# A hybrid decoder layer on one core: the mixers' steps between the projections' half chunks put in another order

## The reference, cut to what matters

```python
h = rmsnorm(x, g_mix_pre)
proj = jnp.einsum('bld,de->ble', h, w_in)                 # 2048 -> 7184 columns
# group B: causal width-4 convolution and SiLU on q, k, v; l2norm of q, k; then, in chunks
A  = jnp.where(strict, bi * jnp.einsum('bhtd,bhsd->bhts', ki, ki) * gam, 0.0)
sol = lax.linalg.triangular_solve(eye + A, rhs, left_side=True, lower=True, unit_diagonal=True)
u  = sol[..., :DV] - jnp.einsum('bhtd,bhde->bhte', sol[..., DV:], S)
S_new = exp(b_last) * S + einsum('bhsd,bhse->bhde', ki * exp(b_last - b), u)
# for the 8 decode tokens the chunk has length 1 and S is one of 8 x 8 stored 128 x 128 states
# group A: gated linear recurrence with a decay per key channel, 8 x 4 stored decode states
x = x + rmsnorm(einsum(concat([oa, ob, oc]), w_out), g_mix_post)
x = x + rmsnorm((silu(h2 @ w_gate) * (h2 @ w_up)) @ w_down, g_ffn_post)
```

## Time and profile before

| | us |
|---|---|
| Median of three runs | 1503.8 |
| The profiled execution: its own time / its span | 1502.13 / 1500.6 |
| PE busy, matmuls (share of the span) | 1423.8 (95%) |
| VectorE busy | 854.1 (57%) |
| ScalarE busy | 661.3 (44%) |
| GpSimd busy | 166.8 (11%) |
| Mean granted TensorE clock | 0.973 of full speed |

### The profile page before, as it was taken

One profiled execution on the slowest core, in us unless ns is written; L12 is line 12 of the kernel. 1 busy time (PEld: TensorE's weight loads), 2 busy tenths in 40 slices (PEclk: granted clock), 3 DMA queues, 4 the chain that ended last, 5 costly groups with the idle time before them and its releaser, 6 DMA issues.

```text
span 1500.6 us, 28229 instructions
## 1 busy us (share of the span) xinstructions
PE 1423.8 (95%) x11389; PEld 1402.2 (93%) x11389; DVE 854.1 (57%) x1123; ACT 661.3 (44%) x839; POOL 166.8 (11%) x196
## 2 busy tenths in 40 slices
PE   6999999999979989896999999999999999999996
PEld 5998999999979989895999999999999999999996
DVE  5757666665557694647655555555555554444444
ACT  6543534435353547445544444444444433343333
POOL 4023132313230301011000000000000000000001
PEclk9999999999999999998999999999999999999998
DMA  6442524425363544552655555555555555554551
GB/s 206 148 141 86 186 85 130 126 84 172 92 193 99 155 118 143 163 185 76 191 178 182 180 181 182 182 182 181 178 180 178 179 182 182 183 182 156 183 169 58
DMA packets 225165, 233.94 MB, mean 156 GB/s; under 512 B 10459, under 2 KB 220414, under 8 KB 224820
## 3 DMA queue, kind: packets, MB, share of 16 engines
q1 hardware_dynamic: 220420, 218.86, 47.2%
q0 software_dynamic: 4672, 14.04, 2.7%
HBM read 223.45 MB, written 9.65 MB: 155 GB/s over the span
## 4 chain that ended last, share of the span: by engine, by line
PE 83%; DVE 9%; ACT 3%; issue 2%; POOL 1%; DMA 1%; SPq 0%; DVEq 0%; ACTq 0%; POOLq 0%
PE ps L604 24%; PE ps L605 24%; PE ps L606 24%; PE ps L740 2%; DVE conv L1535 1%; DVE w_lo L1415 1%; PE ps L746 1%; PE ps L717 1%; PE ps L759 1%; ACT w_hi L1015 1%; PE ps L845 1%; DVE TT L1613 1%; PE ps L626 1%; DVE rs L1617 1%; POOL Ss L522 1%
## 5 line engine op out<-in xcount | busy, mean ns | idle before, releaser
L1415 DVE TENSOR_TENSOR w_lo<-raw,w_hi 128x1024 fp32r<-128x1024 f32 x408 | 504.1, 1237 | 495.2 <-ACT w_hi L1015 494.2
L1015 ACT ACTIVATE w_hi<-raw 128x1024 fp32r<-128x1024 f32 x408 | 431.7, 1059 | 667.2 <-PE ps L606 666.5
L604 PE MATMUL ps<-act_hi,w_hi 128*128 128x264 f32 x2304 | 674.3, 293 | 14.4 <-issue 11.0
L605 PE MATMUL ps<-act_lo,w_hi 128*128 128x264 f32 x2304 | 660.0, 286 | 0.0
L606 PE MATMUL ps<-act_hi,w_lo 128*128 128x264 f32 x2304 | 659.3, 286 | 0.0
L604 PEld LDWEIGHTS ps<-act_hi,w_hi 128*128 128x128 f32 x2304 | 440.8, 191 | 16.4 <-issue 12.4
L605 PEld LDWEIGHTS ps<-act_lo,w_hi 128*128 128x128 f32 x2304 | 441.0, 191 | 0.4
L606 PEld LDWEIGHTS ps<-act_hi,w_lo 128*128 128x128 f32 x2304 | 439.4, 191 | 0.0
L604 PE MATMUL ps<-hid_hi,w_hi 128*128 128x264 f32 x704 | 200.9, 285 | 2.4 <-DVE w_lo L1415 2.4
L605 PE MATMUL ps<-hid_lo,w_hi 128*128 128x264 f32 x704 | 200.9, 285 | 0.0
L606 PE MATMUL ps<-hid_hi,w_lo 128*128 128x264 f32 x704 | 200.7, 285 | 0.0
(11 more groups left out here) (307 smaller groups left out, 1225.2 us busy)
## 6 DMA issues: line engine op xcount, KB each, us to landing
raw<-in_w_in_dram SPq DMA_DIRECT2D x112, 512.0 KB, 3.7
raw<-in_w_gate_dram SPq DMA_DIRECT2D x88, 512.0 KB, 3.5
raw<-in_w_up_dram SPq DMA_DIRECT2D x88, 512.0 KB, 3.5
raw<-in_w_down_dram SPq DMA_DIRECT2D x88, 512.0 KB, 3.4
raw<-in_w_out_dram SPq DMA_DIRECT2D x32, 512.0 KB, 4.6
out_dram<-Ss POOLq DMA_DIRECT2D x12, 512.0 KB, 3.8
Ss<-in_state_gdn_dram POOLq DMA_DIRECT2D x8, 512.0 KB, 6.1
xtok<-in_x_prompt_dram SPq DMA_DIRECT2D x2, 1024.0 KB, 6.0
```

The costliest lines, as they stand in the source:

```text
L604: pe.matmul(out, wh, x_hi[:, kk], start=(kk == begin), stop=False)
L605: pe.matmul(out, wh, x_lo[:, kk], start=False, stop=False)
L1015: return act.activation(out, in_, f, **kw)
L1415: tt(w_lo[:, slot], raw[:, slot], w_hi[:, slot].bitcast(F32), sub).then_inc(lo_done, 1)
```

## The change

- B, TensorE: the key products move from hp 7 to hp 6; the 16 decode products are dealt out by fours over hp 7 to 10; L732 moves from hp 8 to hp 11; the spreads L759 move from hp 14, 16, 18, 20 to hp 15, 17, 19, 21, behind L746.
- A, TensorE: the 16 decode products L851 are dealt out over hp 24, 25 and 26 (6, 5, 5), write another bank, and wait for all eight masked products.
- VectorE: the first two convolutions of a B-kind round are cut in halves of two taps (pos 4 and 5, pos 8 and 9), each behind the mixer's piece; the small decode chain moves from pos 5 to pos 6, behind TT and TM; the copy of A's decode output moves from pos 12 to 13; `state_update` waits for its own four states.
- GpSimd's multiplication of the states goes; ScalarE does it in 16 instructions, four at each of pos 6 to 9 (B) or 4 to 7 (A).
- ScalarE: in rounds of kind "b" the SiLU of a convolution comes behind the mixer's piece.

```diff
 gpsimd, b_mixer (a_mixer likewise, with small[:, 0, :])
-                pool.wait_ge(mx["ld"], 32 * n + 32)
-                pool.wait_ge(mx["ks"], n + 1)
-                pool.wait_ge(mx["pair"], 2 * n + 2)
-                pool.tensor_tensor(Ss[:, :, :], Ss[:, :, :], spair[:, 0, :].unsqueeze(2).broadcast_to([P, 16, P]),
-                                   ALU.mult).then_inc(mx["sdec"], 1)
 tensor, b_step
-                if hp == 6:
+                if 7 <= hp <= 10:
+                    if hp == 7:
                         pe.wait_ge(mx["ld"], 32 * n + 32)
                         pe.wait_ge(mx["tm"], 3 * n + 3)
-                    for x in range(16):
+                    for x in range(4 * hp - 28, 4 * hp - 24):
                         last = pe.matmul(ps[:, 7, 2 * x:2 * x + 2], Ss[:, x, :],
                                          nrm[:, :, x // 8, L + x % 8], start=True, stop=True)
-                    last.then_inc(mx["ks"], 1)
-                if hp == 7:
+                    if hp == 10:
+                        last.then_inc(mx["ks"], 1)
+                if hp == 6:
                     pe.wait_ge(mx["kb"], n + 1)
...
-                if hp == 8:
+                if hp == 11:
                     pe.wait_ge(mx["qkp"], n + 1)
...
-                if hp in (14, 16, 18, 20):
-                    i = (hp - 14) // 2
+                if hp in (15, 17, 19, 21):
+                    i = (hp - 15) // 2
 tensor, a_step
+                if 24 <= hp <= 26:
+                    if hp == 24:
+                        pe.wait_ge(a_["pr"], 8 * k + 8)
+                    for x in range((0, 6, 11)[hp - 24], (6, 11, 16)[hp - 24]):
+                        last = pe.matmul(ps[:, 7, x:x + 1], Ss[:, x, :], q_s[:, x:x + 1], start=True, stop=True)
+                    if hp == 26:
+                        last.then_inc(a_["vs"], 1)
                 if hp == 24:
-                    pe.wait_ge(a_["pr"], 8 * k + 6)
-                    for x in range(16):
-                        last = pe.matmul(ps[:, 4, 256 + x:257 + x], Ss[:, x, :], q_s[:, x:x + 1],
-                                         start=True, stop=True)
-                    last.then_inc(a_["vs"], 1)
 scalar
+            def decay_states(n, i, factor):
+                for x in range(4 * i, 4 * i + 4):
+                    last = A(Ss[:, x, :], Ss[:, x, :], scale=factor[:, x:x + 1])
+                last.then_inc(mx["sdec"], 1)
 b_step
+                if 6 <= pos <= 9:
+                    if pos == 6:
+                        act.wait_ge(mx["ks"], n + 1)
+                        act.wait_ge(mx["pair"], 2 * n + 2)
+                    decay_states(n, pos - 6, spair[:, 0, :])
 a_step (behind the copies v_tm and ke_tm of pos 4)
+                if 4 <= pos <= 7:
+                    if pos == 4:
+                        act.wait_ge(mx["ld"], 32 * n + 32)
+                        act.wait_ge(a_["fs"], k + 1)
+                    decay_states(n, pos - 4, small[:, 0, :])
 vector, b_step: the block "if 6 <= pos <= 11" (TT, TM) now stands ahead of
-                if pos == 5:
+                if pos == 6:
                     dve.wait_ge(mx["ks"], n + 1)
...
-                if i == 0:
-                    dve.wait_ge(mx["sdec"], n + 1)
+                dve.wait_ge(mx["sdec"], 4 * n + i + 1)
 vector, round_
-                    if kind == "b" and pos in (4, 8, 12):
-                        chained[0] = CV * (q - 1)
-                        convolve(3 * r + q - 1, (q - 1) % 2, 3 * CV * r)
+                    if kind == "b" and pos == 12:
+                        chained[0] = 2 * CV
+                        convolve(3 * r + 2, 0, 3 * CV * r)
...
                     mixer(pos)
+                    if kind == "b" and pos in (4, 5, 8, 9):
+                        if pos % 4 == 0:
+                            chained[0] = CV * (q - 1)
+                        convolve(3 * r + q - 1, q - 1, 3 * CV * r, taps=range(2 * (pos % 4), 2 * (pos % 4) + 2))
```

More of the change, by code:

```diff
@@ L518, in a_mixer @@
                 states(n, k, state_hgrn)
[L519 to L523, removed]
                 pool.wait_ge(a_["ex"], 6 * k + 6)
@@ L711, in b_step @@
                     last.then_inc(mx["tr"], 1)
-                if hp == 6:
-                    pe.wait_ge(mx["ld"], 32 * n + 32)
-                    pe.wait_ge(mx["tm"], 3 * n + 3)
-                    for x in range(16):
+                if 7 <= hp <= 10:
+                    if hp == 7:
+                        pe.wait_ge(mx["ld"], 32 * n + 32)
+                        pe.wait_ge(mx["tm"], 3 * n + 3)
+                    for x in range(4 * hp - 28, 4 * hp - 24):
                         last = pe.matmul(ps[:, 7, 2 * x:2 * x + 2], Ss[:, x, :],
                                          nrm[:, :, x // 8, L + x % 8], start=True, stop=True)
-                    last.then_inc(mx["ks"], 1)
-                if hp == 7:
+                    if hp == 10:
+                        last.then_inc(mx["ks"], 1)
+                if hp == 6:
                     pe.wait_ge(mx["kb"], n + 1)
@@ L1217, in round_ @@
                         A(qkv[:, 0], qkv[:, 0], ACT.Silu).then_inc(g_done, 1)
+                    if kind == "c" and pos in (6, 10):
+                        free_qkv(r, q - 1)
+                        silu_conv(12 + q - 1, q - 1, ACT.Copy)
+                    mixer(pos)
                     if kind == "b" and pos in (6, 10, 14):
@@ L1224, in round_ @@
                         silu_conv(3 * r + q - 1, q - 1)
[L1225 to L1228, removed]
                     if prev and pos == 1:
@@ L1521, in after, with convolve @@
                     dve.wait_ge(s, n)
[L1523 to L1526, removed]
+            def convolve(n, slot, base, bias=None, taps=range(CONVW)):
+                if 0 in taps:
+                    dve.wait_ge(raw_q, 2 * n + 2)
+                    after(silu_done, 2 * n)
+                for j in taps:
                     for t in range(2):
@@ L1587, in b_step @@
                     tt(QK[:, :, :], quad(5), decay[:, :, :], mul).then_inc(mx["at"], 1)
-                if pos == 5:
+                if 6 <= pos <= 11:
+                    l = pos - 4
+                    dve.wait_ge(mx["p"], 6 * n + l - 1)
+                    if l == LEVELS - 1:
+                        tt(TM, TM, quad(6), sub).then_inc(mx["t"], 1)
+                    tt(TT[:, :, :], TT[:, :, :], quad(5), sub).then_inc(mx["t"], 1)
+                    if l < LEVELS - 1:
+                        dve.wait_ge(mx["t"], 12 * n + 2 * l - 2)
+                        dve.transpose(TM, TT[:, :, :]).then_inc(mx["t"], 1)
+                if pos == 6:
                     dve.wait_ge(mx["ks"], n + 1)
@@ L1607, in b_step @@
                     tt(oT[:, :, L:T], j2(small[:, 4, :]), j2(small[:, 5, :]), add).then_inc(mx["os"], 1)
[L1608 to L1617, removed]
                 if 7 <= pos <= 10:
@@ L1686, in a_step @@
                             tt(for_j, for_j, sv, mul).then_inc(a_["w"], 1)
[L1687 to L1692, removed]
                 if pos in (8, 9, 10, 11):
@@ L1711, in a_step @@
                             mul, add).then_inc(mx["s2"], 1)
+                    dve.wait_ge(a_["vs"], k + 1)
+                    dve.tensor_copy(oT[:, :, L:T], ps[:, 7, 0:16].rearrange("p (j b) -> p j b", j=2))\
+                        .then_inc(mx["os"], 1)
             CV = 3
```

## The result

The changed kernel takes 1466.68 us (median of four runs, 1464.19 to 1468.30) against 1504.82 for the kernel before on the same chip: ratio 0.9746, 95% interval 0.9733 to 0.9759. The profiled execution took 1466.76 us, its span is 1465.2, so 35.4 less than the span before; the medians differ by more, 38.1, as the profiled execution before (1502.13) was 2.7 us faster than the median here. One run of a later version took 3739.68 us where the five others of that version took 1456.06 to 1460.79; its time is the median of the five. 1465 was forecast. The total is right, but its parts are not: the B rounds gave more than forecast, the A rounds less than half.

The account below looks back on a forecast made before the run. PE, busy 95% of the span, was taken to bound the kernel, through its work, waits and clock. Gains of 23.8 us in B and 14.6 in A, 38.4 together: 1502.1 − 38.4 + 1.7 = 1465.4, said as 1465; range 1455 to 1481.

Parts of the forecast that it names:

- B, decode and key products: Rounds 1 to 4: decode products dealt out, key products first, gain 10.3 us if the clock holds, 0 or less if not.
- B, first position's wait: Convolution moved behind the mixer at the first position: the 4.2 us that L740 waits for GpSimd's AL go.
- B, second position's wait and clock: Convolution behind the mixer at pos 8: waits of 6.2 us and 1.6 of slower clock go, gain 7.8.
- B, spreads: L759 moved behind L746 covers VectorE's TT and TM: 0.9 of short waits and 0.3 us starts, 3.0 taken.
- B, VectorE tight: VectorE at pos 8 nearly level with PE: 1.5 us charged for three rounds, bounds 0 and 6.
- A, round 5: L813's 9.34 us wait for GpSimd goes nearly whole, less new ScalarE waits: net 8.0, bounds 4.3 to 9.3.
- A, round 6: Without GpSimd's multiplication beside `lo`, VectorE is 3.3 us earlier and up to 1.4 more: 3.8 taken, bounds 3.1 to 4.7.
- A, decode products: Dealt out, the chunk behind falls from 4.52 to 2.95 us in both A rounds, less 0.3 for switches: 2.8.
- The step that carried most chance: Dealt-out decode products of B and A rounds keep the clock at 1.00; failure in some rounds 0.08, in all 0.05.
- the rival's case: Clock falls in every dealt-out piece of four B and two A rounds: 44 us more work, 1509 us; chance 0.05.
- The step that failed: Round 5: GpSimd's `kend_f` ready by 441.7, PE arriving at 441.4, so L813's wait goes nearly whole.
- `lo` never at 4 us: Sign for round 6: VectorE's `lo`, stretched to 4.57 instead of 1.24 beside GpSimd's multiplication, no longer takes 4 us.

Follow-up runs that it names:

- a later version: kend_f and nwT on VectorE, group C's convolutions in halves, round 0's whole and ahead, against the changed kernel; 1.07 us wait in round 6; 1458.0 us, 0.9677 to 0.9702.
- the experiment's rounds: Changed kernel with the spreads again beside L730, at hp 14, 16, 18, 20: 1471.43 us; by the rounds' starts the B rounds lose 6.4.
- the experiment's rows: Changed kernel with the 16 one-column decode products of an A round at one place again (hp 24): 1471.28 us.
- the two experiments: Changed kernel with the A rounds' state decay back on GpSimd, 1471.40 us; changed kernel with A's decode products at one place again, 1471.28 us.
- one version: kend_f and nwT on VectorE, round 0's convolutions ahead, group C's first in halves, second whole at position 12, against the changed kernel: 1455.61 us, 0.9675.
- one run: Changed kernel with the A rounds' state decay back on GpSimd as one multiplication of 128x2048: 1471.40 us, 0.9768 to 0.9793.

## Why the prediction was right in sum and wrong in part

| Term | forecast | measured | by |
|---|---|---|---|
| B, decode and key products | 10.3 | 12.2 | 44.5 us in four rounds against 4 × (12.67 − 3 × 1.53) = 32.3 |
| B, first position's wait | 4.2 | 4.2 | wait gone |
| B, second position's wait and clock | 7.8 | 8.1 | 6.2 of waits gone, and round 3, the one with the slow clock, gained 1.9 more than round 2 |
| B, spreads | 3.0 | 6.4 | the experiment's rounds |
| B, VectorE tight | −1.5 | 0 | L730 waits 0.3 in all |
| Round 0 | 0 | −1.5 | L634 waits once more for VectorE |
| A, round 5 | 8.0 | 2.2 | 3.8 less 1.6 for the decode products |
| A, round 6 | 3.8 | 0.5 | 2.1 less 1.6 |
| A, decode products | 2.8 | 3.2 | the experiment's rows |
| Sum | 38.4 | 35.3 | spans: 35.4 |

That 1465 was nearly hit is in part luck: the B rounds gave 7 us more than forecast, the A rounds 9 less, and the 1.7 added at the end for the median covers over half of what the sum falls short, as the changed kernel's profiled execution lies at its median. The split of the A rounds is the least sure: by the rounds' starts of the two experiments it is 3.4, 0.7 and 2.0.

**Clock.** The step that carried most chance held: no dealt-out piece of the changed kernel fell, in six rounds. That the rival's case may be near is seen in one execution of the version with the 1.07 us wait, where the same pieces ran at 0.50. The rule of the Trainium skill that was weighed against the change ("TensorE: Matmul & The Clock Gate", section "A second HAM failure mode: psum-queue depth-cycling") did not come true in the changed kernel: small groups and half chunks in turn ran at 1.00. It was hardly put to the test there, though, since almost no idling is left between them (L730 waits 0.3 us in all).

**A rounds.** The step that failed is "`kend_f` costs 1.25, at worst stretched as the 9.49 is against 3.82, to 3.1: ready by 441.7". The stretch was taken for a ratio. In round 5 it is an absolute delay: GpSimd's operation ends about its own length after VectorE's row does, whether it is 3.8 or 1.25 long. So L803 waited 5.8 us where under 1 was forecast, and L832, the old L842, comes 41.6 us after L793 instead of 43.9, not 8 us sooner:

```profile
436.28 0.39 PE L832 MATMUL ps<-u,nrm 128*128 128x128 f32 x2
```

The rows to see it were there: the 9.49 began at 439.99 and VectorE's row ended at 446.0. What stood before PE in round 5 was the row's end, which the change doesn't move. In round 6 the old kernel's GpSimd had come first, and VectorE's `lo` was the one stretched to 4.57; with the multiplication gone GpSimd comes later, when VectorE's levels have begun, and loses. So "`lo` never at 4 us" came true, and the gain went into a new wait of 5.1 us. The Trainium skill says as much ("SBUF — State Buffer", section "SBUF: two separate sides"): the port pair that the two engines share goes whole to whichever starts first, and the other blocks, for that instruction. The trace agrees that one blocks (1.25 us became 8.50), and goes further: the 14 VectorE operations that started after GpSimd's kept it out one after another.

What VectorE's delay in round 6 had cost PE was also not the 0.66 that the prediction names but mostly one wait for ScalarE, whose exponential had waited for VectorE:

```profile
527.86 1.25 PE L827 MATMUL ps<-masks,small 128*128 128x128 f32 x8 [3.43 <-ACT rs L1015]
```

It is gone, and it is back with 3.4 us where the multiplication is put back on GpSimd.

**Convolution, first position.** The wait went as forecast, but its reason was half of it: with the convolution whole again only 1.8 of the 4.2 us come back, and the rest was covered by the dealt-out products.

**Spreads.** Mis-sized: the 0.3 us starts were counted at 13 places; with the chunk ahead of each L730 the experiment shows some 0.4 at 16. **Round 0** was not walked: the halves behind the mixer delay copies `xT` of VectorE (L634 waits twice, 2.3 us in all, where it waited once, 1.0), though no mixer runs there that could gain by it. ScalarE's decays made no wait in the B rounds (L736, the old L746, waits 0.2 us for ScalarE in all); they take the 30 us of the forecast (20.3 in B, 10.1 in A), while its busy time as a whole rose by 23. GpSimd's busy time fell by 20, not 25 or more: the stretched products fill part of what the multiplications left.

## What to carry to other kernels

When an operation on GpSimd looks stretched, compare its end with the end of VectorE's row beside it, not its length with its length elsewhere: if the difference is its own length, shortening it or removing what stood ahead of it buys only that length, while moving it to VectorE or letting VectorE pause for it takes away the whole wait (here with 5 to 7 us of new ones behind). Take a stall apart by what ends it, before crediting its removal to the instruction that it is listed under. And a forecast that fits in the sum needs its parts checked: here two errors of 7 and 9 us met.

## What was not expected of the hardware

- A wait added to VectorE made the kernel 7 us faster (1466.68 to 1459.83).
- Sixteen decode products in one row brought the clock down behind them and for 3.4 us in three rounds, but within the row and for 6.8 us in the fourth.
- The same dealt-out products ran at 1.00 in the profiled execution of one version and at 0.50 in that of another; ahead of them the rows differ in one wait of 1.07 us.
- GpSimd's operation was kept out by a whole row of VectorE's in round 5, but in round 6 of one run by a single operation.
